# Moving the merge gates' projections into attention, and reordering the filter stage

## The chip, the cores and the metric

The kernel runs on one core of a Trainium2 chip. The metric is the device time of one execution in microseconds (us), shown as the median of the runs given. The engines are PE (TensorE, with its weight loads PEld), DVE (VectorE), ACT (ScalarE), POOL (GpSimd) and SP (SyncE, which issues most transfers). They run their own instruction streams and meet at semaphores.

## What is computed

Two layers (DEPTH = 2) of a hybrid backbone run over 1152 tokens: 1024 latent tokens and 128 context tokens. A layer normalises and modulates its input `h`, projects it once, sends the parts through three token mixers, and merges:

```
proj = h @ p['w_in']
hy_u, hy_z, q, k, v, at_z, pl_u, pl_z, mg = jnp.split(proj, cuts, axis=-1)
y_hy = hyena_branch(hy_u, p) * silu(hy_z)
y_at, kv = attn_branch(q, k, v, ...);  y_at = y_at * silu(at_z)
y_pl = pool_branch(pl_u, p) * silu(pl_z)
r = sigmoid(mg).reshape(B, L, N_BRANCH, D_MODEL)
merged = r[:,:,0]*(y_hy @ w_hy_o) + r[:,:,1]*(y_at @ w_at_o) + r[:,:,2]*(y_pl @ w_pl_o)
out = merged @ p['w_out'];  return x + gate * out
```

D_MODEL is 1024, a mixer is 512 wide, and there are three branches, so `mg` is 3072 columns wide: 24 tiles of 128 channels. Attention is differential: per head (4 of them, two maps of 64 channels each) `w = softmax(s0) - lam * softmax(s1)`, then `w @ v`, then an RMS norm over the head's 128 channels. The hyena mixer multiplies spectra of the input by spectra of filters that a small network makes from the weights alone. `mod = silu(cond) @ w_ada + b_ada` gives the modulation of every layer.

## The kernel before

All tensors lie with channels on the 128 partitions and tokens along the free axis. Every projection of consequence is done in three passes of 32-bit "round" matmuls (fp32r): a weight tile is split into a rounded part `wh` (ACT copies it) and a remainder `wl` (POOL or DVE subtracts), the activations likewise into `hh` and `hl`, and PE adds wh·hh, wh·hl and wl·hh. The helper `project` (L120) does this: a projection tile over K = 1024 is 8 slices x 3 passes x 3 token chunks of 384 columns = 72 matmuls, written with L127.

`build` (L137) runs a phase "start" (L172 on), in which SP loads two constants and copies the input x to scratch memory and waits for all three, then `filters` (L225), and then per layer: `modulated_norm`, `mixers_in`, `values`, two `long_conv`, `attention` (L1530), `branches_out` (L2063), `output` (L2236). Each is a block of its own with a barrier at its end, so nothing overlaps from one to the next.

**`filters`** works through 4 units (2 layers x 2 orders), each of 17 slots. A slot makes one 128-row tile of a spectrum (`spectrum`: 12 matmuls of 512 columns), from a transform matrix tile that SP loads into `draw` (two buffers), ACT rounds into `dh` and DVE subtracts into `dl` (two buffers each). Between the spectra PE makes the taps of the next unit (`hidden_to_taps`), turns the folded taps over (`turn`; DVE writes them in `folds` into two buffers), and does one of 48 `modulation` tiles in each of the slots 1 to 12 (8 products of two columns with a 512 KB weight tile `araw`; 16 matmul records each). SP's order in slot s is: wait for `hout` of the slot before, store that spectrum, load the matrix tile of slot s + 2. ACT's order is: wait for that matrix tile and round it (`matrix_high(m + 2)`), and only then copy the finished spectrum out of PSUM (`spectrum_out(m)`, L704).

**`attention`** runs the heads in a loop. A head has 9 units: 8 tiles of 128 queries against 1280 keys, and one of 128 context queries against 128 keys. For a unit and map c, `scores` (L1683) puts 128 x 1280 scores into banks 0 to 2 (c = 0) or 3 to 5 (c = 1); DVE takes the row maximum (`maximum`, L1976); ACT takes the exponential and its row sum (`softmax`, L1819); DVE inverts the sums and scales the first map (L1986 to L1990), ACT scales the second (`second_map`, L1826), POOL adds them (`combine`, L1914). PE turns the result over in fills of 4, 4 and 2 tiles in bank 6 (`turn`, L1706); ACT rounds each fill (`high`, L1835) and DVE subtracts (`low`, L1996). Every second unit PE multiplies with the values (`with_v`, L1723, 30 matmuls of 256 columns, bank 7), ACT takes the product out (`take`, L1844, L1845), and a short chain over PE, DVE and POOL norms it (`sums`, `means`, `inverse_root`, `spread`, `scale`). The order of step u, written by hand for each engine, is: scores of unit u + 1, then the fills of unit u - 1. At a head's end the next head's keys and queries are split (`split_keys`, `rest_of_keys` L1897, `split_queries` L1962 to L1970) while the last units are finished.

While the first head runs, ACT's queue loads `hh` and `hl`, the projected-from activations, back from scratch (L1883, L1884); attention itself does not read them.

**`branches_out`** takes, per branch, 4 tiles of the silu gate (72 matmuls each, banks 0 to 2 and 3 to 5 in turn) and then, for each of 8 output tiles, the merge gate (72 matmuls, banks 0 to 2) and the output projection of the mixer (K = 512, 36 matmuls, banks 3 to 5). ACT takes the sigmoid of the gate (L2163), DVE multiplies it with the product (L2228) and adds to `merged` (L2233). The gate's and the output's weights come as one tile of 12 slices (768 KB, `w_mo`), split by ACT (L2157) and POOL (L2197).

## Time and profile before

| | us |
|---|---|
| median of 3 runs (4417.24 to 4427.67) | 4418.3 |
| the profiled execution | 4415.23 |
| its span, first to last instruction | 4413.4 |
| PE busy in the span | 3682.9 (83%) |
| DVE busy | 1619.0 (37%) |
| ACT busy | 1157.6 (26%) |
| POOL busy | 981.0 (22%) |
| mean granted clock of PE | 0.906 |

How to read it: a busy time is the sum of the intervals in which an engine had an instruction in flight. Matmuls are pipelined, so a busy PE is not PE at its peak; what a matmul costs in a row of them is the distance from start to start. The granted clock is a share of 2.4 GHz, and 0.5 is 1.2 GHz. A wait is put down to the instruction that released it last. 1.8 us of the profiled execution's time lie outside the span.

### The profile page before, as it was taken

To read this page: it belongs to the slowest core of one execution; us is meant where nothing else is said; L and a number is where in the kernel's file an instruction comes from. 1 tells how busy PE (TensorE), PEld (TensorE's weight loads), DVE (VectorE), ACT (ScalarE), POOL (GpSimd) and SP (SyncE) were. 2 spreads that over 40 slices of the span, in tenths; PEclk is the share of its full clock that TensorE was granted. 3 is DMA by queue.
4 is the path that set the end of the run, shared out by engine and by line. 5 is a ranking of instruction groups with operands and counts; after the bars stand their busy time and mean duration, and the time that the engine had idled before them with its cause. 6 is when DMAs were issued, how large, how long until landed. Compare 5 with 4: busy or idle time off the path is not lost. (4 is left out here: it accounts for less than half of the span.)

```text
span 4413.4 us, 51802 instructions
## 1 busy us (share of the span) xinstructions
PE 3682.9 (83%) x19456; PEld 3354.2 (76%) x19456; DVE 1619.0 (37%) x1938; ACT 1157.6 (26%) x1644; POOL 981.0 (22%) x414
## 2 busy tenths in 40 slices
PE   2888849998885776999999859988776777999999
PEld 2767739986664665999999759876665667999999
DVE  3433333223454665212122153233556662121212
ACT  1323331221111664212121121211115662121211
POOL 2221011120221443222121122211123441212211
PEclk9888879999887887999999979998887888999999
DMA  4565653212565310211111432124563112110204
GB/s 127 181 203 192 199 184 129 80 46 97 207 214 197 93 43 16 78 45 59 50 54 48 179 151 90 46 81 157 209 228 126 48 34 74 38 67 31 74 35 146
DMA packets 177122, 480.55 MB, mean 109 GB/s; under 512 B 32756, under 2 KB 54133, under 8 KB 175638
## 3 DMA queue, kind: packets, MB, share of 16 engines
q1 hardware_dynamic: 175414, 443.47, 29.4%
q10 hardware_dynamic: 1600, 35.65, 2.4%
q8 instruction: 65, 1.06, 0.1%
q14 instruction: 43, 0.35, 0.0%
HBM read 361.92 MB, written 136.86 MB: 113 GB/s over the span
## 5 line engine op out<-in xcount | busy, mean ns | idle before, releaser
L2197 POOL TENSOR_TENSOR branch_wl<-branch_raw,branch_wh 128x1536 fp32r<-128x1536 f32 (+1 forms) x72 | 267.1, 3711 | 926.2 <-ACT branch_wh L2157 926.2
L127 PE MATMUL ps<-hh,branch_wh 128*128 128x384 f32 x1728 | 398.4, 338 | 40.2 <-POOL branch_wl L2197 23.2
L127 PE MATMUL ps<-hl,branch_wh 128*128 128x384 f32 x1728 | 396.8, 337 | 0.0
L127 PE MATMUL ps<-hh,branch_wl 128*128 128x384 f32 x1728 | 396.0, 337 | 0.0
L127 PEld LDWEIGHTS ps<-hh,branch_wh 128*128 128x128 f32 x1728 | 311.3, 190 | 43.6 <-issue 43.6
L2228 DVE TENSOR_TENSOR branch_gate<-ps,branch_gate 128x1152 f32<-128x1152 f32 x48 | 65.2, 1358 | 753.3 <-PE ps L127 753.3
L127 PEld LDWEIGHTS ps<-hl,branch_wh 128*128 128x128 f32 x1728 | 312.2, 190 | 0.0
L127 PEld LDWEIGHTS ps<-hh,branch_wl 128*128 128x128 f32 x1728 | 311.6, 190 | 0.0
L127 PE MATMUL ps<-hh,mixin_wh 128*128 128x384 f32 x720 | 165.8, 338 | 102.3 <-POOL mixin_wl L1106 97.0
L1914 POOL TENSOR_TENSOR attn_prob<-attn_prob 128x1280 f32<-128x1280 f32 (+1 forms) x72 | 190.2, 2641 | 240.0 <-ACT attn_prob L1826 240.0
L1976 DVE TENSOR_REDUCE attn_nmax<-ps 128x1 f32<-128x1280 f32 x144 | 194.6, 1353 | 44.6 <-PE ps L1683 44.4
L127 PEld LDWEIGHTS ps<-hh,mixin_wh 128*128 128x128 f32 x720 | 129.0, 190 | 106.9 <-issue 98.3
L1706 PE MATMUL ps<-ident,attn_prob 128*128 128x128 f32 x648 | 126.2, 314 | 97.6 <-DVE attn_wl L1996 97.1
L2157 ACT CAST branch_wh<-branch_raw 128x1536 fp32r<-128x1536 f32 (+1 forms) x72 | 96.2, 1339 | 381.2 <-PE ps L127 381.1
L1819 ACT ACTIVATE attn_prob<-ps,attn_nmax 128x1280 f32<-128x1280 f32 x144 | 176.1, 1223 | 69.3 <-DVE attn_nmax L1976 53.0
L2163 ACT ACTIVATE branch_gate<-ps 128x1152 f32<-128x1152 f32 x48 | 54.5, 1135 | 526.3 <-PE ps L127 526.3
L1106 POOL TENSOR_TENSOR mixin_wl<-w_in_raw,mixin_wh 128x1024 fp32r<-128x1024 f32 x48 | 115.1, 2400 | 341.4 <-ACT mixin_wh L1031 341.4
L1706 PEld LDWEIGHTS ps<-ident,attn_prob 128*128 128x128 f32 x648 | 84.1, 159 | 124.0 <-DVE attn_wl L1996 90.2
L1031 ACT CAST mixin_wh<-w_in_raw 128x1024 fp32r<-128x1024 f32 x48 | 50.2, 1049 | 482.1 <-DMA w_in_raw<-in_w_in 367.2
L1683 PE MATMUL ps<-attn_kh,attn_qs 128*128 128x512 f32 (+2 forms) x400 | 133.4, 445 | 45.7 <-DVE attn_kl L1968 34.7
L127 PE MATMUL ps<-hl,mixin_wh 128*128 128x384 f32 x720 | 164.9, 336 | 0.0
L127 PE MATMUL ps<-hh,mixin_wl 128*128 128x384 f32 x720 | 164.6, 336 | 0.0
(258 smaller groups left out, 8053.2 us busy)
## 6 DMA issues: line engine op xcount, KB each, us to landing
branch_raw<-in_w_mo SPq DMA_DIRECT2D x48, 768.0 KB
H_dram<-fspec_hout SPq DMA_DIRECT2D x100, 256.0 KB
fspec_araw<-in_w_ada SPq DMA_DIRECT2D x48, 512.0 KB, 4.0
conv_hs<-H_dram SPq DMA_DIRECT2D x32, 768.0 KB, 5.8
w_in_raw<-in_w_in SPq DMA_DIRECT2D x44, 512.0 KB, 3.8
fspec_draw<-in_dft_taps SPq DMA_DIRECT2D x68, 256.0 KB, 3.7
conv_dh<-dft_fwd_kept SPq DMA_DIRECT2D x64, 256.0 KB, 4.2
conv_dl<-dft_fwd_kept SPq DMA_DIRECT2D x64, 256.0 KB, 4.6
```

Of the source, the lines that this page charges most:

```text
L127: last = pe.matmul(out, w[:, k, :], x[:, k, cols], start=(k == 0 and n == 0), stop=(k == kt - 1 and n == 2))
L1031: nc.scalar.copy(wh[:, b], raw[:, b]).then_inc(S["hi"], 1)
L1106: pool.tensor_tensor(wl[:, b], raw[:, b], wh[:, b].bitcast(F32), ALU.subtract).then_inc(S["lo"], 1)
L1683: last = pe.matmul(flat[:, 1536 * c + at:1536 * c + at + width], qs[:, c, q0:q0 + P], keys[:, c, k0 + at:k0 + at + width], start=(m == 0), ...
L1706: last = pe.transpose(ps[:, 6, q * P:(q + 1) * P], prob0[:, u % 3, (at + q) * P:(at + q + 1) * P], ident[:])
L1819: nc.scalar.activation(dst[:, 0:n], flat[:, 1536 * c:1536 * c + n], ACT.Exp, bias=nmax[:, c:c + 1], accum_out=total[:, u % 2, c:c + 1]).th ...
L1914: pool.tensor_tensor(prob0[:, u % 3, 0:n], prob0[:, u % 3, 0:n], prob1[:, u % 2, 0:n], ALU.add).then_inc(S["w"], 1)
L1976: dve.tensor_reduce(nmax[:, c:c + 1], flat[:, 1536 * c:1536 * c + n], AX_X, ALU.max, negate=True).then_inc(S["max"], 1)
L2157: nc.scalar.copy(wh[:, b, 0:size], raw[:, b, 0:size]).then_inc(S["hi"], 1)
L2163: nc.scalar.activation(three(gate[:, b]), banks(0)[:, :, 0:CH], ACT.Sigmoid).then_inc(S["sig"], 1)
L2197: pool.tensor_tensor(wl[:, b, 0:size], raw[:, b, 0:size], wh[:, b, 0:size].bitcast(F32), ALU.subtract).then_inc(S["lo"], 1)
L2228: dve.tensor_tensor(three(gate[:, b]), banks(1)[:, :, 0:CH], three(gate[:, b]), ALU.mult).then_inc(S["p"], 1)
```

## The change

1. **Merge gates.** The 24 merge-gate tiles of a layer are no longer computed in `branches_out`. Each head of `attention` computes 6 of them, in 18 chunks of 384 tokens (24 matmuls each, all into bank 7). `STEP_CHUNKS` says which chunks stand in which step: two in most, one in the steps 3, 5 and 7, where `with_v` stands as well, three after the last. PE issues a chunk in two halves with a `turn` or `scores` between them. ACT takes a chunk out as exp(-x), DVE adds 1 and takes the reciprocal, and SP stores it to the new scratch `gates`. ACT also loads (from its own queue) and rounds the gates' weights, POOL subtracts. The loads of `hh` and `hl`, now needed at once, come slice by slice before the first head.
2. **Attention's order.** A step now does the scores of unit u and the fills of unit u - 1; the loop over heads has no overlap from one head to the next (`split` stands at a head's start). The probabilities are not normalised any more: DVE makes prob0 + ratio * prob1 in one instruction (which replaces its scaling, ACT's `second_map` and POOL's `combine`), and the norm's epsilon is scaled to match. prob0 has 2 buffers instead of 3, prob1 one instead of 2, `wh` and `wl` hold three units.
3. **`branches_out`** loads the finished gates (576 KB for a tile) instead of computing them; the output projections use both bank groups in turn, and the first two of a branch start on three slices before the last slice of `yl` is there.
4. **`filters`.** x is copied to scratch from here instead of in "start". 21 of the 48 modulation tiles run before the first slot, the other 27 in slots 6 to 12 of a unit. Folds are made one slot ahead, in four buffers; `dh` and `dl` have three buffers. Some buffers share memory.

```
 attention, PE (after):
+                    for u in range(1, NU):
+                        cs = STEP_CHUNKS[u]
+                        scores(h, u, 0)
+                        if u in SUMS_OF:
+                            sums(h, SUMS_OF[u])
+                        if u in SPREAD_OF:
+                            spread(h, SPREAD_OF[u])
+                        gate(h, cs[0], 0)
+                        turn(h, u - 1, 0)
+                        gate(h, cs[0], 1)
+                        scores(h, u, 1)
+                        turn(h, u - 1, 1)
+                        if u in PV_OF:
+                            with_v(h, PV_OF[u])
                             turn(h, u - 1, 2)
+                        else:
+                            gate(h, cs[1], 0)
+                            turn(h, u - 1, 2)
+                            gate(h, cs[1], 1)
 attention, PE, one half of a chunk (after); ACT's fev releases the bank:
+                        pe.wait_ge(S["fev"], q + 1)
+                    for k in range(half * KD // 2, (half + 1) * KD // 2):
+                        for n, (w, x) in enumerate(((fwh, hh), (fwh, hl), (fwl, hh))):
+                            last = pe.matmul(ps[:, X_BANK, 0:CH], w[:, j % 2, k, :], x[:, k, (c % 3) * CH:(c % 3 + 1) * CH],
+                                             start=(k == 0 and n == 0), stop=(k == KD - 1 and n == 2))
 attention, ACT:
-                def second_map(h, u):
+                    for u in range(1, NU):
+                        softmax(h, u, 0)
+                        high(h, u - 1, 0)
+                        gate_out(h, cs[0], last)
+                        high(h, u - 1, 1)
+                        softmax(h, u, 1)
+                        if u in PV_OF:
+                            take(h, PV_OF[u])
+                        high(h, u - 1, 2)
+                        if u not in PV_OF:
+                            gate_out(h, cs[1], last)
 attention, DVE:
+                    dve.tensor_scalar(fout[:, c % 2], fout[:, c % 2], 1.0, None, ALU.add).then_inc(S["fone"], 1)
+                    dve.wait_ge(S["fone"], q + 1)
+                    dve.reciprocal(fout[:, c % 2], fout[:, c % 2]).then_inc(S["fr"], 1)
...
+                    dve.scalar_tensor_tensor(out=prob0[:, u % 2, 0:n], in0=prob1[:, 0:n], scalar=to,
+                                             in1=prob0[:, u % 2, 0:n], op0=ALU.mult, op1=ALU.add).then_inc(S["w"], 1)
 branches_out, PE:
-                            project(pe, chunks(banks(0)), wh[:, b], wl[:, b], hh, hl, KD).then_inc(S["g"], 1)
-                            project(pe, chunks(banks(1)), wh[:, b, KD:KO], wl[:, b, KD:KO], yh, yl, CT
-                                    ).then_inc(S["z"], 1)
+                    with pe.Fori(1, KD // 2) as i:
                         for b in range(2):
+                            product(br, 2 * i + b, b, range(CT))
 filters:
-                    sp.dma_start(x_state[0], A["x"]).then_inc(s_in, 16)
+    ADA_AHEAD, ADA = 21, 7
+                    if m >= 3:
+                        act.wait_ge(S["H"], m - 2)
+                    nc.scalar.copy(dh[:, m % 3], draw[:, m % 2]).then_inc(S["dh"], 1)
```

**Where instructions move.** First place: DVE in one step of attention. Before (`attn_rinv` is the pair of inverted row sums, `attn_nmax` the maxima):

```order
L1986 RECIPROCAL attn_rinv<-attn_total 128x2
L72 REGISTER_ALU
L1987 TENSOR_TENSOR attn_rinv<-attn_rinv,attn_lam 128x1
L72 REGISTER_ALU
L1990 TENSOR_SCALAR attn_prob<-attn_prob,attn_rinv 128x1280
L1976 TENSOR_REDUCE attn_nmax<-ps 128x1
L1994 REGISTER_ALU
L1996 TENSOR_TENSOR attn_wl<-ps,attn_wh 128x4x128
L1976 TENSOR_REDUCE attn_nmax<-ps 128x1
```

After, DVE in a step with two chunks, its first half (`attn_fout` is the chunk taken out by ACT):

```order
L2085 TENSOR_REDUCE attn_nmax<-ps 128x1
L2103 REGISTER_ALU
L2105 TENSOR_TENSOR attn_wl<-ps,attn_wh 128x512
L2078 TENSOR_SCALAR attn_fout<-attn_fout 128x384
L2080 RECIPROCAL attn_fout<-attn_fout 128x384
L2083 REGISTER_ALU
L2085 TENSOR_REDUCE attn_nmax<-ps 128x1
```

and its second half, after two more fills of `attn_wl`:

```order
L2093 SCALAR_TENSOR_TENSOR attn_zeps<-attn_total 128x1
L2095 RECIPROCAL attn_ratio<-attn_total 128x1
L72 REGISTER_ALU
L2096 SCALAR_TENSOR_TENSOR attn_ratio<-attn_ratio,attn_lam,attn_total 128x1
L72 REGISTER_ALU
L2099 SCALAR_TENSOR_TENSOR attn_prob<-attn_prob,attn_ratio 128x1280
L2078 TENSOR_SCALAR attn_fout<-attn_fout 128x384
L2080 RECIPROCAL attn_fout<-attn_fout 128x384
```

What moved: a step on DVE has a 384-wide addition and reciprocal between its first fill and its second maximum, and another pair between its combining and the next step's first maximum.

Second place: SP ahead of the first slot of `filters`, before:

```order
L363 DMA fspec_h2h<-fspec_h2h 64x1152 x2
L363 DMA fspec_h2l<-fspec_h2l 64x1152 x2
L367 DMA fspec_h2h<-fspec_h2h 64x1152
L367 DMA fspec_h2l<-fspec_h2l 64x1152
L321 DMA fspec_decay<-in_decay 128x1152 x4
L316 DMA fspec_w<-in_w 64x1024 x2
```

and after:

```order
L370 DMA fspec_h2h<-fspec_h2h 64x1152 x2
L370 DMA fspec_h2l<-fspec_h2l 64x1152 x2
L374 DMA fspec_h2h<-fspec_h2h 64x1152
L374 DMA fspec_h2l<-fspec_h2l 64x1152
L336 DMA fspec_araw<-in_w_ada 128x1024 x5
L326 DMA fspec_decay<-in_decay 128x1152 x2
L336 DMA fspec_araw<-in_w_ada 128x1024 x7
L326 DMA fspec_decay<-in_decay 128x1152 x2
L384 DMA x_state<-in_x 96x12288
L321 DMA fspec_w<-in_w 64x1024 x2
```

What moved: 12 more modulation tiles and the 4.6 MB copy of x stand in SP's queue between the copies of the hidden layer and the first slot.

## Rows read from the trace of the kernel before

**Rows 1.** Stretches (us), busy us of each engine (instructions), granted clock, DMA share, GB/s.
```profile
121.00:599.00 478.00, 414.55 (x2051) 334.47 (x2050) 166.77 (x283) 144.56 (x257) 67.99 (x36) 0.88 0.61 197
1392.00:1764.00 372.00, 255.54 (x1386) 216.73 (x1386) 232.43 (x345) 207.04 (x342) 140.64 (x64) 0.80 0.24 69
1764.00:2392.00 628.00, 607.24 (x3456) 605.52 (x3456) 127.23 (x73) 121.15 (x99) 133.56 (x36) 0.98 0.15 53
```
**Rows 2.** Costliest groups: busy us, mean ns; idle before it and who ended that.
```profile
L127 PE MATMUL ps<-hh,branch_wh 128*128 128x384 f32 x1728 | 398.4, 338 | 40.2 <-POOL branch_wl L2197 23.2 <-ACT branch_gate L2177 17.0
```
**Rows 3.** The stretches again, inside the branch stage: 636 matmuls, nothing else on PE.
```profile
1870.00:1980.00 110.00, 110.00 (x636) 109.77 (x635) 14.14 (x12) 16.83 (x15) 24.77 (x6) 1.00 0.09 31
```
**Rows 4.** Timeline of PE in attention: start us, us, instruction, count.
```profile
1458.58 0.83 PE L1683 MATMUL ps<-attn_kh,attn_qs 128*128 128x512 f32 x3
...
1459.83 0.61 PE L1740 MATMUL ps<-ident,attn_root 128*128 128x128 f32 x4
1460.27 0.60 PE L1706 MATMUL ps<-ident,attn_prob 128*128 128x128 f32 x4
```
**Rows 5.** Timeline of DVE, one unit of attention.
```profile
1459.72 0.15 DVE L1986 RECIPROCAL attn_rinv<-attn_total 128x2 f32<-128x2 f32 x1
1460.23 0.89 DVE L1990 TENSOR_SCALAR attn_prob<-attn_prob,attn_rinv 128x1280 f32<-128x1280 f32 x1 [0.16 <-DVE attn_rinv L1987]
1461.03 1.48 DVE L1976 TENSOR_REDUCE attn_nmax<-ps 128x1 f32<-128x1280 f32 x1
1462.43 0.68 DVE L1996 TENSOR_TENSOR attn_wl<-ps,attn_wh 128x512 fp32r<-128x512 f32 x1
...
1467.19 0.17 DVE L1986 RECIPROCAL attn_rinv<-attn_total 128x2 f32<-128x2 f32 x1
```
**Rows 6.** Timeline of ACT: exponential, its row sum, and a fill.
```profile
1457.67 1.33 ACT L1819 ACTIVATE attn_prob<-ps,attn_nmax 128x1280 f32<-128x1280 f32 x1
1458.99 0.36 ACT L1835 CAST attn_wh<-ps 128x256 fp32r<-128x256 f32 x1
1460.91 0.59 ACT L1835 CAST attn_wh<-ps 128x512 fp32r<-128x512 f32 x1 [1.56 <-PE ps L1706]
```
**Rows 7.** DVE lines: count, ns min/median/max, first and last start, shape.
```profile
L816 DVE RECIPROCAL norm_rstd<-norm_rstd x2: 7353/7353/7353, 625.3 to 2537.5; 128x1152 f32<-128x1152 f32 x2
L1160 DVE RECIPROCAL mixin_roots<-mixin_means x16: 266/266/267, 844.4 to 2904.5; 128x18 f32<-128x18 f32 x16
L218 DVE TENSOR_SCALAR fspec_both<-fspec_both x2: 759/759/759, 30.2 to 43.7; 128x1152 f32<-128x1152 f32 x2
L221 DVE SCALAR_TENSOR_TENSOR fspec_both<-fspec_both x6: 1357/1358/1360, 31.8 to 48.1; 128x1152 f32<-128x1152 f32 x6
```
**Rows 8.** Timelines of DVE and POOL at the first head's start.
```profile
1408.71 4.61 DVE L1965 TENSOR_TENSOR attn_kl<-attn_kraw,attn_kh 128x256 fp32r<-128x256 f32 x1
...
1408.14 4.90 POOL L1897 TENSOR_TENSOR attn_kl<-attn_kraw,attn_kh 128x2048 fp32r<-128x2048 f32 x1 [22.74 <-ACT attn_kh L1803]
```
**Rows 9.** A short stretch in attention, right behind a wait of PE of 2.08 us.
```profile
1443.00:1447.00 4.00, 3.84 (x15) 3.37 (x16) 2.62 (x6) 2.62 (x5) 2.02 (x2) 0.58 0.02 9
```
**Rows 10.** First scores on PE; transfers by line: count, KB each, us to landing.
```profile
1414.18 1.40 PE L1683 MATMUL ps<-attn_kh,attn_qs 128*128 128x512 f32 x3 [6.72 <-DVE attn_kl L1968]
...
hl<-h_keep ACTq DMA_DIRECT2D x2, 4608.0 KB, 23.9
x_state<-in_x SPq DMA_DIRECT2D x1, 4608.0 KB, 16.8
```
**Rows 11.** Timeline of ACT, four slots of the last unit; a transfer and modulations by line.
```profile
566.98 0.58 ACT L704 COPY fspec_hout<-ps 128x512 f32<-128x512 f32 x1
...
589.45 1.06 ACT L704 COPY fspec_hout<-ps 128x512 f32<-128x512 f32 x2
...
fspec_draw<-in_dft_taps SPq DMA_DIRECT2D x68, 256.0 KB, 3.7
L483 PE MATMUL ps<-fspec_scond,fspec_araw 128*128 128x2 f32 x768 | 88.5, 246 | 0.0
```

More of the change, by code:

```diff
@@ L1725, in with_v @@
-                    if half != 0:
-                        last.then_inc(S["pv"], 1)
-                def sums(h, g):
-                    pe.wait_ge(S["o"], NPV * h + g + 1)
-                    for j in range(group(g)[1] // P):
-                        last = pe.matmul(area(G)[:, j:j + 1], sq[:, j * P:(j + 1) * P], ones[:, 0:1], start=True,
+                    us = members(g)
+                    top = max(us)
+                    pe.wait_ge(S["wl"], f_all * h + F_OF[top] + len(fills[top]) + 1)
@@ L1733, in sums @@
+                    last.then_inc(S["pv"], 1)
+                def sums(h, g):
+                    pe.wait_ge(S["o"], NPV * h + g + 2)
+                    if g < NPV - 2:
+                        u = 2 * g + 3
+                        pe.wait_ge(S["wl"], f_all * h + F_OF[u] + 1)
+                    for j in range(len(members(g))):
+                        last = pe.matmul(norm_area(g, G)[:, j:j + 1], sq[:, j * P:(j + 1) * P], ones[:, 0:1], start=True,
                                          stop=True)
@@ L1770, in body @@
-                    if not last:
-                        first_scores(h + 1, 1)
-                    with_v(h, NPV - 2, NU - 2, 1)
-                    if not last:
-                        scores(h + 1, 1, 0)
+                    turn_keys(h)
+                    a, b = STEP_CHUNKS[0]
+                    gate(h, a, 0)
+                    gate(h, a, 1)
+                    scores(h, 0, 0)
+                    gate(h, b, 0)
+                    gate(h, b, 1)
+                    scores(h, 0, 1)
@@ L1780, in body @@
+                    gate(h, b, 1)
                     sums(h, NPV - 1)
+                    gate(h, c, 0)
                     spread(h, NPV - 1)
+                    gate(h, c, 1)
                 pe.wait_ge(S["lexp"], 1)
-                turn_keys(0)
-                first_scores(0, 0)
-                first_scores(0, 1)
-                for c in range(2):
-                    scores(0, 1, c)
-                heads(pe, body)
+                with pe.Fori(0, HEADS) as h:
+                    body(h, False)
@@ L1870, in body @@
-                    if not last:
-                        for c in range(2):
-                            softmax(h + 1, 0, c)
+                    split_keys(h)
+                    a, b = STEP_CHUNKS[0]
+                    gate_out(h, a, last)
+                    softmax(h, 0, 0)
+                    gate_out(h, b, last)
+                    softmax(h, 0, 1)
+                    act.wait_ge(S["v"], 48 * h + 48)
+                    nc.scalar.copy(vh[:], vraw).then_inc(S["vh"], 1)
+                    for u in range(1, NU):
+                        cs = STEP_CHUNKS[u]
+                        softmax(h, u, 0)
[8 more added lines that the diff above has]
+                            gate_out(h, cs[1], last)
@@ L1873, in body @@
+                    a, b, c = STEP_CHUNKS[NU]
                     take(h, NPV - 2)
-                    if not last:
-                        second_map(h + 1, 0)
-                        for c in range(2):
-                            softmax(h + 1, 1, c)
+                    high(h, NU - 1, 0)
+                    gate_out(h, a, last)
                     take(h, NPV - 1)
-                split_keys(0)
-                act.wait_ge(S["v"], 48)
-                act.dma_start(hh[:].bitcast(F32), h_keep[0]).then_inc(S["hin"], 16)
@@ L2120, in _, with product @@
                 pe.sem_inc(S["z"], 2)
+                def product(br, m, b, ks):
+                    if ks[0] == 0:
+                        pe.wait_ge(S["lo"], NW * br + m + CT + 3)
+                        pe.wait_ge(S["p"], KD * br + m + 1)
+                    for k in ks:
+                        if isinstance(m, int) and m < 2:
+                            pe.wait_ge(S["yl"], CT * br + k + 1)
+                        for n, (w, x) in enumerate(((wh, yh), (wh, yl), (wl, yh))):
+                            for out, cols in chunks(banks(b)):
+                                last = pe.matmul(out, w[:, b, k, :], x[:, k, cols], start=(k == 0 and n == 0),
+                                                 stop=(k == CT - 1 and n == 2))
+                    if ks[-1] == CT - 1:
+                        last.then_inc(S["z"], 1)
                 with pe.Fori(0, N_BRANCH) as br:
```

670 lines of the change are left out of this document (356 added, 314 removed).

## The prediction

> **What bounds the kernel now.** I read the stages first, by stretches of the span. Attention takes 372 us per layer, with PE's instructions in flight for 256 of them and a granted clock of 0.80; the branch stage takes 628, with PE busy for 607 at 0.98 [rows 1]. In the branch stage PE is the bound: 636 matmuls of 384 columns in 110 us are 0.173 us each [rows 3], and 3456 of them make 598 of the 628 us [rows 1]. PE waits there for ACT's taking out of a gate for 17.0 us in two layers, and once per layer for the first weights [rows 2]. Attention is a ring of several engines, in which none is full: a unit takes 7.5 us from one reciprocal to the next [rows 5], while PE's part is two scores of 1.25, about 0.9 of fills and half of a value product (30 matmuls of 256 columns, at two thirds of 0.173 each 3.5 us). So the change takes work from the stage with no room and puts it where PE has gaps. What counts is what the other engines need for it, and how long a step becomes.
>
> **The branch stage.** It loses 24 tiles of 72 matmuls: 1728 x 0.173 = 299 us per layer. The waits for ACT's gate are lost too, since the first products now start on three slices: 17.0 / 2 = 8.5. The gates' loads (576 KB per 6.2 us, with 256 KB of weights) ask for about 137 GB/s, below the 197 that the filters hold for 478 us [rows 1], and POOL's and ACT's split of a 512-wide tile is shorter than the 36 matmuls (6.2 us) it hides behind. Cost nothing; if this cover fails, each tile waits on its gate. **-307.5 us per layer.**
>
> **A step of attention after.** Prices, from start to start:
>
> - PE: a chunk 24 x 0.173 = 4.15 (half: 2.08); scores of a map 1.25, a fill of four 0.4, as the four matmuls in front of it (0.44) [rows 4]; value product 3.5.
> - DVE: maximum 1.40 (in flight 1.48, so neighbours overlap by 0.08), fill of 512 columns 0.68 - 0.08 = 0.60 [rows 5], of 256 columns by the same slope 0.34.
> - ACT: exponential with its sum 1.32, fill 0.59 or 0.36 [rows 6].
> - The new reciprocal of 384 columns is not in the trace. 18 columns take 0.266 us and 1152 take 7.353, which is 6.25 ns a column: 2.55 us for 384 [rows 7]. Its ends are these two rows; the line between them is straight enough that I take 2.55 and allow 0.3.
> - The addition of 1: 759 ns for 1152 columns [rows 7], so 0.3. With the reciprocal behind it 2.8 us a chunk, 72 chunks a layer.
> - The combining on DVE: 1358 ns for 1152 columns [rows 7], so 1.5 for 1280, and 0.55 for the three small ones before it, as between the reciprocal and the scaling now [rows 5]: 2.05.
>
> On DVE a two-chunk step holds 2 x 1.40 + 2 x 0.60 + 0.34 + 2.05 + 2 x 2.8 = 12.0 us of work. PE's part is 2 x 1.25 + 2 x 4.15 + 0.9 + 0.3 = 12.0 as well. Neither fills the step, because two places of DVE's order wait for something that begins only when the instruction in front is done. (a) `low(u-1, 0)` needs ACT's `high`, which stands behind `softmax(u, 0)`, which needs the maximum just taken: 1.32 + 0.59 and latency, 2.07 us idle. (b) `low(u-1, 2)` stands behind `softmax(u, 1)` in the same way: 1.32 + 0.36 less the 0.60 that the fill in front covers, 1.25 idle. PE is ahead at both. So 12.0 + 2.07 + 1.25 = **15.3 us**. A step with the value product has one chunk less and ACT's `take` (0.6) in front of the last fill: 15.3 - 2.8 + 0.6 = **13.1**.
>
> A head: four two-chunk steps 61.3, three with the value product 39.3, the small context unit with its two chunks 9 (bound by PE). Then PE alone: value product, three chunks, small unit and norms, with about 2 us of waiting for the norm: 21. Then the head's start. From the last chunk's end to the last of its queries DVE needs 0.6 + 2.8 + 6.4 us, of which its subtraction of the keys waits for POOL, as today (4.61 us for a 256-wide instruction while POOL's runs) [rows 8]. Then come chunk, maximum, chunk, maximum, combining: 22 in all up to the first combining. Sum 61.3 + 39.3 + 9 + 21 + 22 = 152.6.
>
> The clock: behind a wait of 2.08 us the granted clock was 0.58 over 4 us [rows 9], that is near the lower level of 1.2 GHz. In the new two-chunk step PE waits 1.1 and 2.4 us. Half a chunk at the lower level costs 12 x 0.147 = 1.8 more, and 1.0 of it reaches DVE. I add 4 us a head, **156.6**; between nothing and 10.
>
> The stage's start: scores begin at 1414.2 now, 22 us in [rows 10]. The change needs 2.6 MB of queries and keys and then 9.4 MB of `hh` and `hl` before its first chunk is done; those 9.4 MB land 23.9 us after their issue [rows 10]. That puts the first scores at about 38 us in, 29.5 us after what stands for a previous head's end. End of the last head to the block's end: 5.5. Attention: 29.5 + 4 x 156.6 + 5.5 = 661, against 372: **+289 us per layer.**
>
> Here a page bears on the reciprocal. The three rows say 6.25 ns a column [rows 7]. The Trainium skill, "VectorE: DVE Perf Modes", section "First, the fixed hardware budget", says that it runs the divide with a repeat count of 8. By eight times the 1.18 ns a column of a plain two-input instruction 384 columns would take 3.6 us, and the sum would be 1.07 x 144 = 154 us worse; the measured row decides against that here.
>
> **The filters.** The wait for x in "start" goes (16.8 us for its copy [rows 10], less about 2 for the constants): -15. Ahead of the first tap PE now has four modulation tiles whose loads SP issues behind the copies of the hidden layer, three at a time: +8. Eight more stand between the turns: +5. The copy of x is in the same queue just ahead of slot 2's matrix: +5. The slots themselves take 478 us, 7.0 each [rows 1]. In the last unit, where PE has no taps, four slots without modulation still take 22.5 us, 5.6 each [rows 11]. This is a ring: hout of slot m-1, SP's stores and load, 3.7 us to landing [rows 11], ACT's rounding, and only then hout of slot m. A third `dh` doesn't open it. So 5.6 is a floor: 68 x 1.4 = 95 us would be the most. The 21 modulations that leave the slots (88.5 / 48 = 1.8 us each [rows 11], 39 in all) and the folds' waits are part of that; I take -35, between 0 and -75. **Filters -32.**
>
> **Sum.** 2 x (289 - 307.5) - 32 = -37 - 32 = -69. 4415.2 - 69 = 4346 against the profiled execution; the median of the runs stands 3 us above it, less than can be told. I give **4346 us**. (A measurement of this kernel tells 0.3%, 13 us, from no change.)
>
> **The rivals.**
>
> 1. *The ring is looser than I think, and PE or DVE is full.* Then a two-chunk step is 12.0 and a head about 125. For it: both have 12.0 us of work. Against it: waits (a) and (b) follow from the written order, and today's unit takes 7.5 us with 5.2 of PE. It gives 8 x 30 = 240 less: **4105**. Chance 0.13.
> 2. *The clock becomes the bound (slower).* The place is PE in the two-chunk steps. At a granted clock of 0.65, PE's 12.0 us become 18.5. Over seven steps and eight heads that is 3.2 x 56 = 179 us above the forecast: **4525**. It decides from the point where a step costs 1.2 us more (69 / 56), which is a clock of 12.0 / 16.5 = 0.73 in those steps. For it: 0.80 over the stage now, and 0.58 behind a wait [rows 1, 9]. Against it: PE's share of the step rises from 5.2 of 7.5 to 12 of 15.3. Chance 0.12.
> 3. *POOL holds DVE up (slower).* An instruction of DVE with two inputs in SBUF took 4.61 us until POOL's was done [rows 8]. POOL now subtracts 24 gate tiles a layer, by that row 2.4 us for 1024 columns, while DVE combines and adds 1. If each of the 48 is paid in full, 115 us: **4461**; break-even at 29 of them. Against it: they start behind a chunk, where DVE is in the reciprocal or the maximum. The rule behind it is in the Trainium skill, "GPSIMD Engine Reference", section "1. Specifications": the SBUF interface is shared with VectorE where that has two SBUF inputs or a 2-port mode. Chance 0.08.
> 4. *The gain doesn't appear.* Heads of 165 us, or filters that only lose their prologue's gain: 4400 to 4430. Chance 0.10.
>
> **How the numbers follow.** The forecast has 0.57, with a range of its own from 4270 to 4420 (a head of 150 to 163, filters from 0 to -75). Faster: 0.13 + 0.57, less 0.02 for its upper end, 0.68 + 0.02 of the others = 0.70. Same: 0.09. Slower: rivals 2 and 3 and a part of 4, 0.21. The range leaves out rival 1 and the worst of rival 2: **4240 to 4470**.
>
> **What would show it.** In the new profile: a branch stage of 320 us per layer with 1728 matmuls at 0.173; an attention stage of 640 to 690; reciprocals of 384 columns at 2.5 us; DVE idle in front of the first fill of a unit, released by ACT's fill, about 2 us; a slot pace in the filters of 6.3 to 6.6, still with ACT waiting for the matrix. A step of 12 us, a reciprocal of 3.6, or a granted clock under 0.75 in attention would each make it wrong.

## The result: 4485 us, 1.4% slower

| | before | after |
|---|---|---|
| median | 4422.7 us | 4485.5 us |
| ratio, 95% interval | | 1.0144 (1.0117 to 1.0171) |
| profiled execution: its time, span | 4415.2, 4413.4 | 4486.9, 4485.2 |
| ahead of the normalization's first matmul, one time | 605.5 | 594.5 |
| attention, layer 0 and 1 | 372.6, 371.1 | 710.8, 716.3 |
| branch stage, per layer | 628 | 328.4 |

The forecast was 4346. By the spans the change costs 72 us where I expected a gain of 69. I take the 141 us between the two apart by the same stages.

The stages after, as in [rows 1]: busy us of each engine (instructions), granted clock, DMA share, GB/s; the last line is layer 1.

```profile
1378.80:2089.60 710.80, 547.99 (x3114) 508.54 (x3114) 466.93 (x525) 224.80 (x402) 107.74 (x52) 0.91 0.24 74
2089.60:2418.00 328.40, 305.89 (x1728) 303.05 (x1728) 115.12 (x73) 62.17 (x67) 63.04 (x36) 0.97 0.32 106
3324.40:4040.70 716.30, 551.11 (x3114) 511.98 (x3114) 466.93 (x525) 224.76 (x402) 107.67 (x52) 0.90 0.24 73
```

The branch stage gives back 299.6 us, the 1728 matmuls at 0.173 and nothing else. Attention takes 338 and 345 us more for them. PE was idle in 116 of attention's 372 us [rows 1] and is now idle in 163 of 711: the gaps took in none of the 299 us of chunks on balance, and VectorE's busy time went from 232 to 467.

VectorE in attention of layer 0, the costliest lines with the idle time ahead of them:

```profile
L2080 DVE RECIPROCAL attn_fout<-attn_fout 128x384 f32<-128x384 f32 x72 | 183.8, 2553 | 2.5
...
L2105 DVE TENSOR_TENSOR attn_wl<-ps,attn_wh 128x512 fp32r<-128x512 f32 (+2 forms) x100 | 58.5, 585 | 115.8 <-ACT attn_wh L1941 115.8
...
L2078 DVE TENSOR_SCALAR attn_fout<-attn_fout 128x384 f32<-128x384 f32 x72 | 25.8, 358 | 80.3 <-ACT attn_fout L1905 80.2
```

The reciprocal is the 2.55 us read off [rows 7]. The 115.8 us ahead of the low parts are waits (a) and (b), 29 a head. The 80.2 us are waits for ACT's taking out of a chunk, 20 a head. In the steps my forecast had no such wait; the first head has 6.8 us of it there and 1.3 in the small unit, and the rest lies in the tail and at the head's start. One two-chunk step of VectorE, from one combining to the next (as [rows 5]: start us, us, instruction, idle before it and who ended it):

```profile
1448.55 1.55 DVE L2099 SCALAR_TENSOR_TENSOR attn_prob<-attn_prob,attn_ratio 128x1280 f32<-128x1280 f32 x1
1450.78 0.36 DVE L2078 TENSOR_SCALAR attn_fout<-attn_fout 128x384 f32<-128x384 f32 x1 [0.68 <-ACT attn_fout L1905]
1451.17 2.55 DVE L2080 RECIPROCAL attn_fout<-attn_fout 128x384 f32<-128x384 f32 x1
1453.64 1.43 DVE L2085 TENSOR_REDUCE attn_nmax<-ps 128x1 f32<-128x1280 f32 x1
1457.04 0.69 DVE L2105 TENSOR_TENSOR attn_wl<-ps,attn_wh 128x512 fp32r<-128x512 f32 x1 [1.96 <-ACT attn_wh L1941]
1457.64 0.35 DVE L2078 TENSOR_SCALAR attn_fout<-attn_fout 128x384 f32<-128x384 f32 x1
1458.03 2.55 DVE L2080 RECIPROCAL attn_fout<-attn_fout 128x384 f32<-128x384 f32 x1
1460.50 1.43 DVE L2085 TENSOR_REDUCE attn_nmax<-ps 128x1 f32<-128x1280 f32 x1
1461.84 0.68 DVE L2105 TENSOR_TENSOR attn_wl<-ps,attn_wh 128x512 fp32r<-128x512 f32 x1
1463.68 0.42 DVE L2105 TENSOR_TENSOR attn_wl<-ps,attn_wh 128x256 fp32r<-128x256 f32 x1 [1.16 <-ACT attn_wh L1941]
...
1464.53 1.55 DVE L2099 SCALAR_TENSOR_TENSOR attn_prob<-attn_prob,attn_ratio 128x1280 f32<-128x1280 f32 x1
```

16.0 us: the forecast's 15.3 with its waits of 1.96 and 1.16, and 0.68 more for a chunk that was late. It is one of the shorter ones. The first head's four two-chunk steps take 16.0, 15.8, 17.1 and 18.3 (67.0 for the forecast's 61.3), its three one-chunk steps 13.6, 13.4 and 13.5 (40.4 for 39.3). Why the chunk was late stands on PE, whose second half of that chunk came behind a wait of 1.90 us for a fill and ran partly at half speed (the starts go from 0.17 apart to 0.32):

```profile
1446.55 0.44 PE L1794 MATMUL ps<-ident,attn_prob 128*128 128x128 f32 x2 [1.90 <-DVE attn_wl L2105]
...
1447.17 0.34 PE L1753 MATMUL ps<-hh,attn_fwl 128*128 128x384 f32 x1
1447.35 0.35 PE L1753 MATMUL ps<-hh,attn_fwh 128*128 128x384 f32 x1
...
1449.38 0.52 PE L1753 MATMUL ps<-hl,attn_fwh 128*128 128x384 f32 x1
1449.70 0.52 PE L1753 MATMUL ps<-hh,attn_fwl 128*128 128x384 f32 x1
```

The first head against the forecast. The tail runs to the end of the last chunk on PE (1576.9), where the forecast begins the next head's start:

| part | forecast | measured | what is in the difference |
|---|---|---|---|
| unit 0 to unit 7 | 100.6 | 107.5 | VectorE waits 6.8 for late chunks, in seven places; smaller differences cancel |
| small unit | 9 | 12.6 | VectorE waits 3.3 for a fill behind a chunk, 1.3 for a chunk |
| tail | 21 | 21.9 | PE sets the pace, as forecast |
| next head's start | 22 | 27.7 | VectorE's split of queries and keys takes 11.0, not 6.4 |
| clock | 4 | (above) | |
| sum | 156.6 | 169.7 | |

13 us a head are 105 of the 141. The split runs from 1580.29, where the rounding of the queries takes 5.19 us beside GpSimd (last section), to 1591.33. PE waits for it ahead of the next head's first scores:

```profile
1590.31 1.40 PE L1776 MATMUL ps<-attn_kh,attn_qs 128*128 128x512 f32 x3 [8.25 <-DVE attn_kl L2069]
```

In the first head of the kernel before, the same five instructions took 9.4 us, from the start of the first of these rows to the end of the last. The last three of them, from the 4.61 us of [rows 8] on, took 6.6, which is near the forecast's 6.4:

```profile
1405.93 1.36 DVE L1958 CAST attn_qs<-attn_qraw 128x2304 fp32r<-128x2304 f32 x1 [11.53 <-DMA attn_craw<-in_cache_k]
...
1413.95 1.35 DVE L1970 TENSOR_TENSOR attn_qs<-attn_qraw,attn_qs 64x1152 fp32r<-64x1152 f32 x1
```

### The profile page after: what moved, and what is told of

Read it like the earlier page. It is cut to its first block and busy times, and to the rows that moved or that the text cites. A ratio compares the mean times of both kernels' runs of the same rounds, so it can differ in the third digit from the quotient of the medians.

```text
span 4485.2 us, 53438 instructions
## 1 busy us (share of the span) xinstructions
PE 3701.7 (83%) x19456; PEld 3371.2 (75%) x19456; DVE 2068.0 (46%) x2294; ACT 1068.8 (24%) x1695; POOL 775.1 (17%) x390
## 5 line engine op out<-in xcount | busy, mean ns | idle before, releaser
L1753 PE MATMUL ps<-hh,attn_fwh 128*128 128x384 f32 x1152 | 430.2, 373 | 16.8 <-DMA hl<-h_keep 11.1
L1753 PE MATMUL ps<-hh,attn_fwl 128*128 128x384 f32 x1152 | 409.3, 355 | 0.0
L1753 PE MATMUL ps<-hl,attn_fwh 128*128 128x384 f32 x1152 | 408.0, 354 | 0.0
L2080 DVE RECIPROCAL attn_fout<-attn_fout 128x384 f32<-128x384 f32 x144 | 367.6, 2553 | 5.0
L1753 PEld LDWEIGHTS ps<-hh,attn_fwh 128*128 128x128 f32 x1152 | 233.3, 202 | 24.1 <-DMA hl<-h_keep 11.9
L1794 PE MATMUL ps<-ident,attn_prob 128*128 128x128 f32 x648 | 115.8, 294 | 161.2 <-DVE attn_wl L2105 91.8
L1753 PEld LDWEIGHTS ps<-hl,attn_fwh 128*128 128x128 f32 x1152 | 233.9, 203 | 0.0
L2007 POOL TENSOR_TENSOR attn_fwl<-attn_fraw,attn_fwh 128x1024 fp32r<-128x1024 f32 x48 | 121.4, 2530 | 649.0 <-ACT attn_fwh L1898 649.0
L1753 PEld LDWEIGHTS ps<-hh,attn_fwl 128*128 128x128 f32 x1152 | 232.6, 202 | 0.0
L2299 POOL TENSOR_TENSOR branch_wl<-branch_raw,branch_wh 128x512 fp32r<-128x512 f32 (+1 forms) x72 | 126.2, 1757 | 524.1 <-ACT branch_wh L2272 524.1
L127 PE MATMUL ps<-hh,branch_wh 128*128 128x384 f32 x576 | 134.2, 341 | 39.4 <-POOL branch_wl L2299 39.4
```

What stands on the lines that cost most here:

```text
L127: last = pe.matmul(out, w[:, k, :], x[:, k, cols], start=(k == 0 and n == 0), stop=(k == kt - 1 and n == 2))
L1753: last = pe.matmul(ps[:, X_BANK, 0:CH], w[:, j % 2, k, :], x[:, k, (c % 3) * CH:(c % 3 + 1) * CH], start=(k == 0 and n == 0), stop=(k == K ...
L1794: last = pe.transpose(ps[:, T_BANK, q * P:(q + 1) * P], prob0[:, u % 2, (at + q) * P:(at + q + 1) * P], ident[:])
L2007: pool.tensor_tensor(fwl[:, b], fraw[:], fwh[:, b].bitcast(F32), ALU.subtract).then_inc(S["flo"], 1)
L2080: dve.reciprocal(fout[:, c % 2], fout[:, c % 2]).then_inc(S["fr"], 1)
L2299: pool.tensor_tensor(wl[:, b, 0:size], raw[:, b, 0:size], wh[:, b, 0:size].bitcast(F32), ALU.subtract).then_inc(S["lo"], 1)
```

## The experiments

The ratio stands against runs of the kernel before on the same chip, whose median was 4423.3 (e1 to e4), 4423.8 (e5 to e8), 4433.3 (e9 to e11) and 4427.3 (e12).

### e1: the new filters with the old attention and branches

Attention, branches and the stages around them are taken from before; start, filters and the copy of x from after.

> The filters, the start and the x copy as changed; attention and branches as before. In the changed kernel's trace the normalization starts 11 us earlier than before (589.1 against 600.3), attention plus branches take 1039 us a layer against 1000. If the stages add up, this kernel takes 4418 - 11 = 4407 (within 0.3% of before), and attention with the branches carries all of the loss. If the filters' loads or the late copy of x cost something later that the stage marks hide, it is slower than before, 4425 or more.

Measured: 4399.5 us, 0.9951 (0.9929 to 0.9973). The filters alone gain 22 us. The moved projections therefore lose 4485.5 - 4399.5 = 86. A little faster than expected, not slower: no cost of the late copy of x shows.

### e2: tanh on ACT in place of VectorE's division

```diff
-  nc.scalar.activation(fout[:, c % 2], ps[:, X_BANK, 0:CH], ACT.Exp, scale=-1.0)
+  nc.scalar.activation(fout[:, c % 2], ps[:, X_BANK, 0:CH], ACT.Tanh, scale=0.5)
...
-  dve.tensor_scalar(fout[:, c % 2], fout[:, c % 2], 1.0, None, ALU.add).then_inc(S["fone"], 1)
-  dve.wait_ge(S["fone"], q + 1)
-  dve.reciprocal(fout[:, c % 2], fout[:, c % 2]).then_inc(S["fr"], 1)
+  dve.tensor_scalar(fout[:, c % 2], fout[:, c % 2], 0.5, 0.5, ALU.mult, ALU.add).then_inc(S["fr"], 1)
```

The gate is the same function, 0.5 + 0.5 tanh(x/2).

> Theory D (VectorE's chain sets the step: 2.9 us of addition and reciprocal per chunk lie on it): with 0.36 us a chunk instead, 2.55 x 144 = 367 us leave VectorE. PE's own 12.0 us of a two-chunk step then bound it, so I expect 13 instead of 16 for such a step, a head of 140 to 148 instead of 169.8, and 4240 to 4310 in all. Theory P (PE, through its clock or its order, sets the step): a head of 163 or more, 4430 or more.

Measured: **4235.5 us, 0.9569 (0.9553 to 0.9585)**, 250 us less than the change and faster than both kernels. Attention of layer 0 and one head in it:

```profile
1375.20:1961.80 586.60, 514.91 (x3114) 489.00 (x3114) 291.75 (x453) 227.40 (x402) 108.02 (x52) 0.95 0.30 89
1429.40:1567.30 137.90, 128.22 (x778) 121.90 (x778) 73.10 (x112) 56.41 (x101) 27.17 (x13) 0.98 0.27 79
```

A head takes 138 us with PE in flight for 128 of them, where it took 169.7; the step shown above takes 11.9 (the first head's other two-chunk steps 13.6, 13.9 and 14.0). So the division with its addition was the cost, and PE's order could absorb the chunks once VectorE came in time. The step shows what is left: both of the waits (a) and (b) are still there, and lie beside PE's work now.

```profile
1439.28 1.55 DVE L2097 SCALAR_TENSOR_TENSOR attn_prob<-attn_prob,attn_ratio 128x1280 f32<-128x1280 f32 x1
...
1444.74 0.69 DVE L2103 TENSOR_TENSOR attn_wl<-ps,attn_wh 128x512 fp32r<-128x512 f32 x1 [1.96 <-ACT attn_wh L1941]
...
1450.30 0.42 DVE L2103 TENSOR_TENSOR attn_wl<-ps,attn_wh 128x256 fp32r<-128x256 f32 x1 [1.15 <-ACT attn_wh L1941]
...
1451.15 1.55 DVE L2097 SCALAR_TENSOR_TENSOR attn_prob<-attn_prob,attn_ratio 128x1280 f32<-128x1280 f32 x1
```

### e3: a third of the chunks' matmuls left out

```diff
-  for n, (w, x) in enumerate(((fwh, hh), (fwh, hl), (fwl, hh))):
+  for n, (w, x) in ((0, (fwh, hh)), (2, (fwl, hh))):
```

> The chunks' middle product (high weights by the low part of the input) is left out: 8 of 24 matmuls, 1.39 us per chunk at 0.173 each, 200 us of PE's work over both layers. Theory P: all of it is given back, 4285. Theory D: PE has slack in the steps, and only what reaches VectorE comes back: its waits for a chunk's taking out (about 1 us in each of seven steps, 2.3 us at four places of a head's end and start), 10 to 13 us a head: 4380 to 4410.

Measured: 4422.8 us, 0.9996 (0.9984 to 1.0008). Of 200 us of PE's work 63 come back. That is 13 short of theory D's range and far from theory P's 4285. Attention with 576 matmuls fewer, at a lower granted clock than the change's 0.91:

```profile
1373.40:2053.50 680.10, 463.15 (x2538) 421.00 (x2538) 470.99 (x525) 224.19 (x402) 107.92 (x52) 0.87 0.25 77
```

VectorE's wait for chunks falls from 80.2 to 49.6 us in the stage, 30.6 less, which is what the stage loses (710.8 to 680.1).

### e4: the whole chunk ahead of the first fill

```diff
   gate(h, cs[0], 0)
-  turn(h, u - 1, 0)
   gate(h, cs[0], 1)
+  turn(h, u - 1, 0)
```

> PE does the whole of a step's first chunk ahead of the first fill, where the second half stood behind it. Theory: VectorE's wait for this chunk's taking out (0.7 to 1.2 us in seven of eight steps) comes from that half, which stands behind the fill and so behind the combining. With the order turned it goes, if the first fill isn't late in its place: 0.8 x 8 x 8 = 50 us less, 4435. Rival: the first half alone filled PE's wait for the combining, and the second now delays the fill by as much: 4480 to 4500.

Measured: 4458.1 us, 1.0072 (1.0054 to 1.009), 27 less than the change: the effect is there at half its size. VectorE's waits in attention of layer 0, to be set beside 80.2 and 115.8 above:

```profile
DVE attn_wl L2105 <- ACT attn_wh L1941: 126.9, 68, 3.8
DVE attn_fout L2078 <- ACT attn_fout L1905: 54.9, 30, 5.4
```

25 us of one wait go, 11 come back in the other.

### e5: GpSimd's subtraction cut to an eighth

```diff
-  pool.tensor_tensor(fwl[:, b], fraw[:], fwh[:, b].bitcast(F32), ALU.subtract).then_inc(S["flo"], 1)
+  k = slice(0, KD) if isinstance(t, int) and t == 0 else slice(0, 1)
+  pool.tensor_tensor(fwl[:, b, k], fraw[:, k], fwh[:, b, k].bitcast(F32), ALU.subtract).then_inc(S["flo"], 1)
```

> GpSimd subtracts only 128 of the 1024 columns of each gate weight tile after the first; the rest of the low parts keeps old values, so the chunks' third product is not the reference's. PE, ACT and VectorE do the same instructions. Theory D: in the changed kernel's trace GpSimd's subtraction stretches VectorE only at a head's start (3.38 us for a 64x1152 subtraction that takes 1.35 elsewhere): 2 us a head, at most 16 in all, 4470 to 4485. Theory G (the port is what costs: each of the 48 subtractions holds VectorE up by up to its 2.4 us): 4370 to 4420.

Measured: 4467.7 us, 1.0094 (1.0076 to 1.0111): 18 us less, 2 past the edge of theory D and far from G. Attention is shorter by 3 and 5 us of these. VectorE's subtraction of the queries had a median of 3377 ns and has

```profile
L2066 DVE TENSOR_TENSOR attn_qs<-attn_qraw,attn_qs x8: 1356/1491/1493, 1403.5 to 3863.9; 64x1152 fp32r<-64x1152 f32 x8
```

The rest of the 18 lies in stages that the edit doesn't touch; the marks of stages vary by some us from kernel to kernel. The keys' subtraction on GpSimd stays in e5, and so does the 5.19 us of the rounding beside it: theory D's share of GpSimd was tested in part only.

### e6: VectorE's division moved into its wait

```diff
   gate(h, cs[0], 0)
-  turn(h, u - 1, 0)
   gate(h, cs[0], 1)
+  turn(h, u - 1, 0)
...
+  gate_out(h, cs[0], last)
   softmax(h, u, 0)
   high(h, u - 1, 0)
-  gate_out(h, cs[0], last)
...
-  low(h, u - 1, 0)
   sigmoid(h, cs[0])
+  low(h, u - 1, 0)
```

> The same instructions in another order on three engines: PE does the whole first chunk of a step ahead of the first fill, ACT takes it out ahead of the exponential, and VectorE adds and divides before the first low part, so that this lies in the 2 us in which it waited for ACT's fill. If the step is VectorE's 12.05 us of work plus the waits that its order makes, a two-chunk step falls from 16 to 13.5 and a one-chunk step from 13.5 to 11, 15 to 20 us a head: 4330 to 4370. If PE's 12 us of work with its own waits for the fills bind instead, under 8 us a head: above 4420.

Measured: 4523.9 us, 1.0219 (1.0199 to 1.0238), 38 us *slower* than the change and 66 slower than e4, which has the same order on PE. Neither theory had this. VectorE in a two-chunk step, and the bounds of a one-chunk step later on:

```profile
1448.86 1.55 DVE L2099 SCALAR_TENSOR_TENSOR attn_prob<-attn_prob,attn_ratio 128x1280 f32<-128x1280 f32 x1
...
1458.49 0.63 DVE L2105 TENSOR_TENSOR attn_wl<-ps,attn_wh 128x512 fp32r<-128x512 f32 x1
1459.04 1.48 DVE L2085 TENSOR_REDUCE attn_nmax<-ps 128x1 f32<-128x1280 f32 x1
1460.49 0.69 DVE L2105 TENSOR_TENSOR attn_wl<-ps,attn_wh 128x512 fp32r<-128x512 f32 x1
1463.87 0.42 DVE L2105 TENSOR_TENSOR attn_wl<-ps,attn_wh 128x256 fp32r<-128x256 f32 x1 [2.69 <-ACT attn_wh L1941]
...
1464.73 1.55 DVE L2099 SCALAR_TENSOR_TENSOR attn_prob<-attn_prob,attn_ratio 128x1280 f32<-128x1280 f32 x1
...
1481.48 1.55 DVE L2099 SCALAR_TENSOR_TENSOR attn_prob<-attn_prob,attn_ratio 128x1280 f32<-128x1280 f32 x1
...
1495.86 1.55 DVE L2099 SCALAR_TENSOR_TENSOR attn_prob<-attn_prob,attn_ratio 128x1280 f32<-128x1280 f32 x1
```

and PE in that one-chunk step:

```profile
1490.12 0.66 PE L1794 MATMUL ps<-ident,attn_prob 128*128 128x128 f32 x4 [2.49 <-DVE attn_wl L2105]
```

The wait of 1.96 us ahead of the first low part is gone, and the one ahead of the third grew from 1.16 to 2.69, with waits of about 1 us for the chunk as before. All three fills of a unit go through one bank: PE may turn the next only when VectorE has the low part of the last. With the division ahead of the first low part the second fill starts later, and PE stands still: its waits for a low part went from 46.5 to 91.7 us in the stage. The two-chunk step takes 15.9 us, no more than in the change: what the one wait gives the other takes. The one-chunk step takes 14.4 where it took 13.4, and the first head in all 173.1 for 169.7. The wait was not free time that work could be put into. It was a piece of a loop over PE, ACT and VectorE. e6 changes the order on all three at once, so how much of the 38 each order costs is not shown.

### e7, e8, e11: the parts of the filters

Three kernels, each the changed one with one edit. e7 has 12 modulations ahead of the slots and 9 in a unit:

```diff
-    ADA_AHEAD, ADA = 21, 7
+    ADA_AHEAD, ADA = 12, 9
```

with its loads and the modulations between the turns cut to match. e8 gives the third matrix buffer up:

```diff
-  if m >= 3:
-      act.wait_ge(S["H"], m - 2)
-  nc.scalar.copy(dh[:, m % 3], draw[:, m % 2]).then_inc(S["dh"], 1)
+  if m >= 2:
+      act.wait_ge(S["H"], m - 1)
+  nc.scalar.copy(dh[:, m % 2], draw[:, m % 2]).then_inc(S["dh"], 1)
```

and the same in `matrix_low` and in PE's `spectrum`. e11 puts VectorE's folds back:

```diff
-  if n + 1 < NU:
-      for ct, f in even_groups(s + 1):
-          if f < 4:
-              folds(n + 1, ct, f)
...
+  for ct, f in even_groups(s):
+      if f < 4:
+          folds(n + 1, ct, f)
```

> 12 modulations ahead of the slots instead of 21, and 9 instead of 7 in a unit's slots. In the changed kernel's trace a modulation in the prologue is 1.75 us of PE at the low clock, in line with everything else: nine fewer give 16 to 20 us. The nine go into the slots, where PE waits for the matrix anyway: 0 to 13 us. Net -3 to -20: 4465 to 4482. If the slots pay in full for each, no change or slower.

> The third buffer of the rounded matrix is given up again (two, with the old waits); folds and modulations stay as changed. The prediction said that the third buffer opens nothing, since ACT waits there for the matrix's landing and not for PE: 4480 to 4490. Rival: ACT's waits for PE (31.7 us in the slots of before, gone after) were real and the buffer removed them: 4505 to 4520.

> VectorE folds in the slot in which PE turns the taps, as before, not one slot ahead; the four fold buffers, the third matrix buffer and the modulations stay as changed. The slots of the changed kernel take 438 us, 40 less than before. Neither the third buffer nor nine modulations more changed that. If the folds' place is what gave it, this kernel is 25 to 40 us slower: 4510 to 4525. Rival: it is all in the modulations that left for the prologue and their loads' queue: no change, 4480 to 4490.

Measured: e7 4475.5 us, 1.0116 (1.0096 to 1.0135), 10 less. e8 4487.5 us, 1.0145 (1.0129 to 1.0161), no difference: no gain of the third buffer shows. e11 4519.5 us, 1.0196 (1.0178 to 1.0214); its runs of before were slower too, so by the ratios it is 0.5% or 23 us slower than the change. The stage mark says the same: the normalization's first matmul, in the change and in e11.

```profile
594.49 17.32 PE L811 MATMUL ps<-norm_sq,ones 128*128 128x384 f32 x48 [9.86 <-ACT norm_sq L821]
```

```profile
617.39 17.66 PE L810 MATMUL ps<-norm_sq,ones 128*128 128x384 f32 x48 [9.80 <-ACT norm_sq L820]
```

So the place of the folds gives about 22 of the 38 us by which the slots got shorter; the other 16 I did not take apart. One mark is not exact: seven other kernels here with the change's filters have it between 586.4 (e4) and 592.9 (e6), so the 594.5 of the change is the latest of them. For e7 I had a modulation at 1.75 us in the prologue. The rows of the change say otherwise (a tile is 16 matmuls):

```profile
25.10 6.99 PE L433 MATMUL ps<-fspec_scond,fspec_araw 128*128 128x2 f32 x32 [1.17 <-DMA fspec_araw<-in_w_ada]
...
63.82 13.81 PE L433 MATMUL ps<-fspec_scond,fspec_araw 128*128 128x2 f32 x64 [14.24 <-DMA fspec_araw<-in_w_ada]
...
105.72 6.82 PE L433 MATMUL ps<-fspec_scond,fspec_araw 128*128 128x2 f32 x32
```

3.45 us a tile, nearly twice the 1.84 of a tile in the slots. In e7 the first spectrum began at 125.0 instead of 146.5, 21.5 us earlier for nine tiles, and its slots took 454.5 us instead of 448.0. That is 0.7 us for each of the nine, no more than the slots of one and the same kind differ by (438 in e4, 448 in the change).

### e9, e10, e12: faster versions, and the head's start

e9 is e2 with both chunks of a head's start ahead of the scores; e10 adds the edit of e7; e12 adds to that ACT's earlier rounding of the keys.

```diff
   gate(h, a, 0)
   gate(h, a, 1)
-  scores(h, 0, 0)
   gate(h, b, 0)
   gate(h, b, 1)
+  scores(h, 0, 0)
   scores(h, 0, 1)
```

```diff
   gate_out(h, b, last)
+  if not last:
+      round_keys(h + 1)
   gate_out(h, c, last)
```

(`round_keys` is the first half of `split_keys`, to the second copy into `kh`.)

> The tanh kernel with one more edit: at a head's start PE does both chunks ahead of the first scores. In the tanh kernel's trace PE waits 4.4 us per head there for VectorE's low part of the keys, and works at the lower clock behind it; the second chunk, 4.2 us, now lies in this wait. 4 to 6 us a head: 4187 to 4205. Rival: VectorE's split of queries and keys stands behind the last chunk and sets the head's start whatever PE does; then the chain split, scores, maximum, exponential is as long as before and only the chunk behind it goes, under 2 us a head: above 4220.

> The same with the 12 modulations ahead of the slots of the run before. That edit gave 10 us to the changed kernel; the stages are apart, so it should give the same here: 5 to 15 us less than the kernel beside it, 4175 to 4195.

> The fastest kernel so far with one more edit: ACT rounds the next head's keys ahead of the last chunk's taking out, not behind it, so that GpSimd subtracts them (5.5 us in the fastest kernel's trace) 5 us earlier and VectorE's subtraction of the keys, which took 4.7 us beside it, is short. PE's waits at a head's start were 0.7, 1.8 and 2.3 us there. If the chain ACT, GpSimd, VectorE sets the head's start, 3 to 5 us a head: 4175 to 4192. Rival: the start hangs on VectorE's split behind the last chunk, which stays: under 1 us a head, 4205 or more.

Measured: e9 4233.9 us, 0.9553 (0.9534 to 0.9572), no difference to e2 that can be told. **e10 4214.6 us, 0.9517 (0.9497 to 0.9537)**, 19 less than e9 beside it. e12 4213.1 us, 0.9513 (0.9487 to 0.9538), no gain over e10. In e9 the stretch from the small unit's combining to the next head's first fell from 42.7 to 39.8 us, but the stage's own start got 4 us longer, since the first head's scores now stand behind two chunks. In e10 PE's one long wait was split into several:

```profile
1537.26 0.84 PE L1772 MATMUL ps<-attn_kh,attn_qs 128*128 128x512 f32 x3 [0.74 <-DVE attn_qs L2067]
1540.50 0.84 PE L1772 MATMUL ps<-attn_kh,attn_qs 128*128 128x512 f32 x3 [1.82 <-ACT attn_prob L1927]
1546.31 1.11 PE L1790 MATMUL ps<-ident,attn_prob 128*128 128x128 f32 x4 [2.30 <-DVE attn_prob L2093]
```

In e12 GpSimd's subtraction of the keys came earlier and ran beside one of VectorE's multiply-adds, and its subtraction of the gate's weights ran beside another; each otherwise takes 0.36 us:

```profile
1536.93 2.06 DVE L2079 TENSOR_SCALAR attn_fout<-attn_fout 128x384 f32<-128x384 f32 x1 [2.19 <-ACT attn_fout L1901]
...
1544.13 2.44 DVE L2079 TENSOR_SCALAR attn_fout<-attn_fout 128x384 f32<-128x384 f32 x1
```

The head's start is a chain of split, scores, maximum, exponential and combining behind the last chunk. Taking one piece out shortens it by 1 us or less a head.

## Why the prediction was wrong

**What bounds the kernel** was read rightly for each stage. The conclusion "puts it where PE has gaps" was not: those gaps are waits inside a loop, and they grew as the chunks came in (116 to 163 us idle), because each chunk brings 2.9 us to VectorE in the same loop. With 0.36 us a chunk in its place (e2) PE is idle for 72 us.

**The branch stage, -307.5.** Measured -299.6. The 1728 matmuls are right to the tenth; the gain of 8.5 beside them failed. PE was idle for 21 of 628 us and is idle for 22 of 328. The waits for ACT's gate are gone, but the wait for the first weights grew from 11.6 to 15.3, and seven short waits for GpSimd's split, 8.9 us, are new: "cost nothing" was wrong for it. 16 us over two layers.

**The step.** The prices held: reciprocal 2.553, addition 0.36, 12.05 us of work on VectorE in a two-chunk step, wait (a) 1.96 for 2.07, wait (b) 1.16 for 1.25. The step that failed is the sentence "PE is ahead at both". It held at (a) and (b), but at two other places of VectorE's order, its additions, PE is not ahead: the second half of a chunk stands behind a fill, which waits for the combining or the last low part, and part of that half runs at half speed. In the first head that is 7 us in the steps and part of 3.6 in the small unit, against the 4 that I had added for the clock. e3 and e4 bear on it: less work per chunk, or none behind the fill, cuts this wait (80.2 to 49.6 and 54.9). A second term was sized wrong: VectorE's split at a head's start, 6.4 in the forecast and 11.0 measured. The rounding of the queries and their first subtraction run beside GpSimd there and take 5.19 and 3.38 us, where both took 1.36 in the first head of before. No experiment takes this term alone; e5 shortens the 3.38. In all 169.7 for 156.6, **105 of the 141 us**.

**The reciprocal, row against page.** The measured 2.553 us is [rows 7] to the last digit, not the 3.6 that came from the repeat count (the Trainium skill, "VectorE: DVE Perf Modes", section "First, the fixed hardware budget"). What I did not draw from it: at 2.9 us with the addition, 2.6 of them were avoidable, and e2 shows them worth 250 us.

**The filters, -32.** Measured -11 by the stage marks, which lie late in this one trace, and -22 by e1. The slots were right (-38 by the marks, -30 with the copy of x in the forecast), and so was "a third `dh` doesn't open it" (e8). The prologue failed: -15 + 8 + 5 became +27, since a modulation there takes 3.45 us and not the 1.8 of [rows 11], and sixteen of them, 8 ahead of the first tap and 8 between the turns, come to 55 us, of which the old wait for the hidden layer covers only a part.

**The rivals.** Rival 4, "heads of 165 us, or filters that only lose their prologue's gain", named both failures, but stopped at 4430. Rival 2 fell: the granted clock in attention was 0.91, not 0.65 to 0.73. Its seed was real, half-speed halves behind waits, at a few us a head. Rival 3 fell: e5 gives 18 us at most. In the change's trace GpSimd's 48 subtractions of gate weights met reciprocals and maxima, which kept their times, and none of the 64 combinings; only the head's start paid. So the rival fell by where the subtractions stand. What a combining would take that starts behind one, no run shows. Rival 1, steps of 12, is what e2 comes near with 11.9 to 14.0, and it takes the division away.

**The size of the bet.** The forecast for attention and branches was +289 against -307.5: a gain of 18 us a layer between two numbers of 300. Each chunk costs 4.7 us in attention (342 / 72) and saves 4.16. An error of 6% in either term, which the steps' latencies alone make, turns the sign; 0.70 for faster was too much.

## What to carry to other kernels

Idle time of an engine inside a loop of several engines is not room: before work is moved there, write down the loop, and count what the moved work adds to each of its engines, above all to the one whose instructions others wait for. If it brings an elementwise step, choose its form first: here tanh on ACT and one multiply-add for an exponential, an addition and a reciprocal turned +1.4% into -4.3%. When the forecast is the difference of two large terms, set the chances by their errors and not by its sign.
